# Gated delta heads: another order of the head loop, and the 16x16 block inversion on GpSimd

## The reference, cut to what matters

```
q, k, v = silu(causal conv, width 4, of the projected q, k, v);  q, k unit-norm
decay   = exp(gc_i - gc_j)                     # gc: running sum of the log decay
A       = strict_lower((beta k) k^T * decay)   # in chunks
T       = inverse(I + A)
u = T (beta v);   w = T (beta k exp(gc));   attn = (q k^T) * decay
for each chunk:   v_new = u_c - w_c S
                  o_c   = (q_c exp(gc_c)) S + attn_c v_new
                  S     = S exp(g_last) + (k_c exp(g_last - gc_c))^T v_new
o = gated RMSNorm(o) * silu(z)
```

## Time and profile before

| | |
|---|---|
| median of 3 runs | 2806.33 us (2804.72 to 2807.24) |
| the profiled execution | 2806.93 us, of which the trace's span is 2805.1 us |
| mean granted TensorE clock | 0.915 |
| busy, share of the span | PE 85%, PEld 78%, DVE 40%, ACT 23%, POOL 0.2 us |
| DMA | 191.38 MB, 68 GB/s |

### The profile page before, as it was taken

The page is one execution under the profiler, slowest core; times in us unless marked ns, Lnnn a source line. Parts: engine busy times, 40 slices in busy tenths (PEclk is TensorE's granted clock), DMA queues, the critical chain, the costliest instruction groups (busy, mean ns, idle before and its releaser), DMA issues. The chain is left out here.

```text
span 2805.1 us, 34802 instructions
## 1 busy us (share of the span) xinstructions
PE 2397.6 (85%) x13800; PEld 2184.2 (78%) x13800; DVE 1115.0 (40%) x1922; ACT 638.7 (23%) x1174; POOL 0.2 (0%) x4
## 2 busy tenths in 40 slices
PE   5898985778889898898889667979799999979998
PEld 3686974578878888797878555967699999977676
DVE  4132312535656465655656453334322222231133
ACT  3122312013223131323223110025211111121221
POOL 0000000000000000000000000000000000000000
PEclk9999996579999999999999956989899999989999
DMA  4010210321111111101110044443322222132341
GB/s 153 0 63 16 71 46 16 122 55 50 32 49 38 34 48 32 57 22 50 31 49 16 20 144 140 150 154 113 88 67 67 67 74 68 53 134 54 107 122 57
DMA packets 224158, 191.38 MB, mean 68 GB/s; under 512 B 30253, under 2 KB 197198, under 8 KB 224047
## 3 DMA queue, kind: packets, MB, share of 16 engines
q1 hardware_dynamic: 212792, 152.71, 18.8%
q10 hardware_dynamic: 11302, 37.82, 3.4%
HBM read 138.57 MB, written 52.11 MB: 68 GB/s over the span
## 5 line engine op out<-in xcount | busy, mean ns | idle before, releaser
L271 PE MATMUL bank<-xT_hi,w_lo 128*128 128x344 f32 x1152 | 399.4, 347 | 3.8 <-DVE w_lo L267 3.8
L272 PE MATMUL bank<-xT_lo,w_hi 128*128 128x344 f32 x1152 | 374.1, 325 | 0.0
L273 PE MATMUL bank<-xT_hi,w_hi 128*128 128x344 f32 x1152 | 373.4, 324 | 0.0
L271 PE MATMUL bank<-xT_hi,ffn_lo 128*128 128x344 f32 x1056 | 338.4, 320 | 11.9 <-DVE ffn_lo L267 11.9
L273 PE MATMUL bank<-xT_hi,ffn_hi 128*128 128x344 f32 x1056 | 337.8, 320 | 0.0
L272 PE MATMUL bank<-xT_lo,ffn_hi 128*128 128x344 f32 x1056 | 337.3, 319 | 0.0
L271 PEld LDWEIGHTS bank<-xT_hi,w_lo 128*128 128x128 f32 x1152 | 223.5, 194 | 6.0 <-issue 6.0
L272 PEld LDWEIGHTS bank<-xT_lo,w_hi 128*128 128x128 f32 x1152 | 223.0, 194 | 1.9 <-issue 1.9
L273 PEld LDWEIGHTS bank<-xT_hi,w_hi 128*128 128x128 f32 x1152 | 222.1, 193 | 0.0
L271 PEld LDWEIGHTS bank<-xT_hi,ffn_lo 128*128 128x128 f32 x1056 | 199.2, 189 | 11.9 <-issue 11.9
L273 PEld LDWEIGHTS bank<-xT_hi,ffn_hi 128*128 128x128 f32 x1056 | 199.1, 188 | 0.0
(11 more groups left out here) (377 smaller groups left out, 4158.2 us busy)
## 6 DMA issues: line engine op xcount, KB each, us to landing
w_raw<-in_w_in SPq DMA_DIRECT2D x48, 512.0 KB, 3.9
ffn_raw<-in_w_ffn_in SPq DMA_DIRECT2D x44, 512.0 KB, 5.0
act_scr<-ffn_y ACTq DMA_DIRECT2D x22, 516.0 KB, 2.7
fo_sr<-act_scr SPq DMA_DIRECT2D x16, 704.0 KB, 6.7
fo_wr<-in_w_ffn_out SPq DMA_DIRECT2D x22, 512.0 KB, 5.1
gate_scr<-gate ACTq DMA_DIRECT2D x16, 516.0 KB, 3.7
a_kv_raw<-in_w_in SPq DMA_DIRECT2D x3, 2048.0 KB, 8.6
mix_ta<-gate_scr SPq DMA_DIRECT2D x8, 516.0 KB, 4.8
```

Source lines behind the costliest of these rows:

```text
L271: nc.tensor.matmul(out, stat_lo, mov_hi, start=start, stop=False)
L272: nc.tensor.matmul(out, stat_hi, mov_lo, start=False, stop=False)
L273: return nc.tensor.matmul(out, stat_hi, mov_hi, start=False, stop=stop)
```

## The change

1. **The table and the tiles' order.** `per_slot` becomes 10, 2, 3, 3, 44, 4, three times 6, 4, 2, eight times 4, 18, 4, again 144 steps in sum. The tiles of a head in the loop come as a, q, k, v, b, z. The first tile's weights of the next head are split at the end of the head before (`lo(h + 1, 0)`, `hi(h + 1, 0)`).
2. **The inversion** moves from DVE to GpSimd, with its 28 operations and memset unchanged; GpSimd also clears `ub` at the start. SP's queue has `base_to` ahead of the head's fourth weight load and `base_from` ahead of the sixth.
3. **The norms and the rows.** The squares' sums of q and of the output are taken by ACT (`accum_out`, eight small operations each) in place of DVE's products and sums. The four rb banks come from 16 transposes of a broadcast column in place of four 512-wide products with a diagonal made by DVE, so DVE's two `diag` products go. "an" is made before the last of the four bounds. ACT's tables are loaded ahead by name.
4. **Banks and waits.** The levels' first products use two banks (6, 5) in place of one; the scan has one step in place of two between m1 and m3; `state` is cleared before the levels; `on` comes in two halves; the z silu and `pt` stand later.

```diff
-            per_slot = [20, 4, 8, 8, 28] + LEVELS * [6] + [4] + NT * [4] + [14, 8]
+            per_slot = [10, 2, 3, 3, 44, 4] + LEVELS * [6] + [4, 2] + NT * [4] + [18, 4]
...
-                return 0, NTILE
+                return {0: "a", 1: "q", 2: "k", 3: "v", 4: "b", 5: "z"}
...
                 for n in range(4):
-                    src = (kbe if n < 2 else kdec)[:, 4 * (n % 2):4 * (n % 2) + 4]
-                    inc(nc.tensor.matmul(banks[4 + n][:], ident_ones[:], src.rearrange("p a b -> p (a b)"),
-                                         start=True, stop=True), "rb")
+                    for p in range(4):
+                        c = col[:, 4 if n < 2 else 2, 4 * (n % 2) + p:4 * (n % 2) + p + 1]
+                        last = nc.tensor.transpose(banks[4 + n][:, p * P:(p + 1) * P], c.to_broadcast([P, P]),
+                                                   ident[:])
+                    inc(last, "rb")
...
-                            last = nc.tensor.matmul(banks[6][:, p * P:(p + 1) * P], ea[:, 4 * b + p],
+                            last = nc.tensor.matmul(banks[x_bank[b]][:, p * P:(p + 1) * P], ea[:, 4 * b + p],
                                                     t_sb[b][:, p], start=True, stop=True)
...
-                    fill.upto(done[SCAN + c] - 2)
+                    fill.upto(done[SCAN + c] - 3)
...
-                    inc(nc.scalar.activation(sqb[:].rearrange("p a b -> p (a b)"), banks[5 + b][:],
-                                             ACT.Square), "q_ev")
+                    for p in range(4):
+                        x = banks[5 + b][:, p * P:(p + 1) * P]
+                        last = nc.scalar.activation(x, x, ACT.Square, accum_out=col[:, 1, 4 * b + p:4 * b + p + 1])
+                    inc(last, "q_ev")
...
-                fill.upto(done[BASE] - 16)
-                invert_base(v, nc.vector, i)
...
+                @block.gpsimd
+                def _(pool):
+                    nc.gpsimd.memset(ub[:], 0.0).then_inc(cleared, 1)
+                    with pool.Fori(0, HB) as i:
+                        invert_base(pool, nc.gpsimd, i)
```

More of the change, by code:

```diff
@@ L1781, in project_pe @@
             def project_pe(pe, h, prev):
-                for m in range(*turn_tiles(h)):
+                for m in turn_tiles(h):
                     j, u = m % 2, m // 2
@@ L1796, in project_act, with hi @@
             def project_act(act, h, prev):
-                def hi(m):
+                kind, first, end, more = bounds(h)
+                def hi(h, m):
                     j, u = m % 2, m // 2
@@ L1858, in project_act, with lo @@
                         yield n + 3 * KT
[L1859 to L1860 removed]
+                        hi(h, m + 2)
+                    elif m + 2 == end and more:
+                        yield n + 3 * KT
+                        hi(h + 1, 0)
+                    if x in CONVS:
+                        c = CONVS.index(x)
                         wait(act, evac[2], h, m + 1)
[L1862 to L1863 removed]
+                        inc(nc.scalar.activation(conv_new[:, bass.ds(c * HB + h, 1)],
+                                                 pre[c][:, L:L + 3 + NS].unsqueeze(1), ACT.Copy), "cn")
             def project_dve(v, h, prev):
[L1866 removed]
+                kind, first, end, more = bounds(h)
+                def lo(h, m):
                     j, u = m % 2, m // 2
@@ L2091, in recur_act @@
                     inc(nc.scalar.activation(qe[:, 512 * b:512 * b + 512], banks[6 + b][:], ACT.Exp), "qe_x")
-                for b in range(2):
-                    wt(act, "eq_m", i, b + 1)
                     inc(nc.scalar.activation(eq[:, 4 * b:4 * b + 4], eq[:, 4 * b:4 * b + 4], ACT.Exp), "eq_x")
-                fill.slot(3)
+                wait(act, silu, i, 3); wait(act, evac[2], i, 6)
+                nc.scalar.activation(tanh[:], z_half[:], ACT.Tanh).then_inc(thalf.sem, 1)
                 fill.upto(done[BASE])
@@ L2151, in recur_dve, with bounded @@
                 wt(v, "cols", i, 1)
-                for dst, c in ((kbe, 4), (kdec, 2)):
-                    inc(nc.vector.tensor_tensor(dst[:], ident[:].unsqueeze(1).to_broadcast(F8),
-                                                col[:, c].unsqueeze(2).to_broadcast(F8), ALU.mult), "diag")
-                wait(v, thalf, i, 4)
-                wt(v, "ob", i, 0)
-                nc.vector.scalar_tensor_tensor(zs[:], tanh[:], 1.0, z_half[:], ALU.add,
-                                               ALU.mult).then_inc(silu.sem, 1)
-                fill.slot(2)
-                for n in range(4):
-                    if n == 2:
-                        v.wait_ge(out_dma, 16 + i * 16)
+                def bounded(n):
                     wt(v, "rb", i, n + 1)
@@ L2216, in recur_dve @@
                         w_t[:, 4 * b:4 * b + 4],
-                        banks[4 - b][:].rearrange("p (a b) -> p a b", a=4)), "w_ev")
-                v.wait_ge(st_dma, 16 + i * 16)
-                inc(nc.vector.memset(state[0][:], 0.0), "sm")
+                        banks[3 + b][:].rearrange("p (a b) -> p a b", a=4)), "w_ev")
+                fill.slot(APPLY + 1)
                 wt(v, "u_ev", i, 2)
@@ L2282, in _ @@
                 def _(v):
-                    nc.vector.memset(ub[:], 0.0).then_inc(cleared, 1)
                     constants_take(v)
```

227 lines of the change are left out of this document (119 added, 108 removed).

## The result

The changed kernel takes 2632.5 us (median of 4 runs, 2629.1 to 2636.9), the kernel before 2805.6 in the same session (2804.7 to 2807.2). The ratio is 0.9383, with a 95% interval of 0.9366 to 0.9400. The prediction was 2688 with a range of 2646 to 2775: the direction was right, and the gain of 173 us was half as large again as the 118 forecast. The profiled execution took 2634.9 us, span 2633.2.

A forecast was written before the change was run, and what follows sets the result against it. PE's queue, its work plus its own waits, was taken as the bound. Six loop heads save 91.2 us, the first 9.8, the last 17.2: 118.2 off 2806.93 gives 2688.7, predicted as 2688, range 2646 to 2775.

The forecast's parts named there:

- Which waits go: PE's waits in loop head: silu of v 3.79, bounds 1.18 and `state` 0.92 us gone; levels' 3.45 cut to 0.5.
- The way of the blocks: Inversion's round trip from head start: `base` in place at 20.7 us, X 12.5, 7.0 back; PE's filler ends at 37.1.
- X: Time of the inversion on GpSimd: 12.5 us, the geometric middle of 6.35 (DVE's time) and 24.
- rival 2: GpSimd and DVE hinder each other, adding some 2.5 us to the inversion (X = 15); 2712 us, chance 0.15.
- the clock loss: Behind PE's 3.1 us wait for `ub` in a loop head, half clock loses 1.6 more: 4.7 together.
- rival 1: The 44 steps cover the whole inversion, X at or below 9.4, a head 106.5 us; 2649 us, chance 0.17.
- PE's bare head: PE's loop head without any wait: 105.0 us, from 126.4 less 16.4 waits, 3.7 clock and 1.3 rb.
- The levels (0.5) and the scan (1.0): PE's waits left in a loop head: 0.5 us (0 to 3) in levels, 1.0 (0.3 to 3) in scan.
- The last head: Last head, without filler: 17.2 us saved; 12.9 at the turned blocks, 0.9 `state`, about 2 levels, 1.4 output's norm.
- rival 3: Fillers' new place makes DVE late in levels or scan, 3 us more wait a head; 2709 us, chance 0.10.
- rival 4: Inversion on GpSimd bounds a head, each us of X costing 8 in all; 2864 us at X = 34, slower part 0.06.
- my signs of being wrong: PE waits for `col` at rb, m3 for `vnew` in over four chunks, or GpSimd operations stretch where DVE is busy.

The follow-up runs named there:

- Run 7: Changed kernel with the tiles again in the old order a, b, q, k, v, z: 2691.4 us.
- run 4: Changed kernel with DVE's products for `kbe` and `kdec` moved from beside GpSimd's inversion to just before the first level: 2624.6 us.
- run 5: Changed kernel with six, and in a second kernel fourteen, extra dependent 64x56 products on GpSimd ahead of each inversion: 2678.2 and 2719.7 us.
- run 6: Changed kernel with both halves' first products of the levels sharing bank 6 again, the second waiting for the first's mask: 2640.8 us.
- run 8: Changed kernel with the levels' filler steps back in their old place on PE and DVE, both banks kept: 2640.3 us.
- run 9: Changed kernel with one bank for the levels' first products and the levels' filler steps in their old places, both at once: 2673.4 us.
- Run 1: Changed kernel with the inversion back on DVE, behind the weight split of filler step 24: 2624.5 us.
- run 3: Changed kernel with 47 filler steps in place of 44 ahead of the turned blocks and 15 in place of 18 in the tail: 2624.5 us.
- run 11: Changed kernel with the inversion on DVE, ahead of the products for `kbe` and `kdec`: 2620.5 us.
- run 10: Changed kernel with 42, or 40, filler steps in place of 44 ahead of the turned blocks and 20, or 22, at the head's end: 2653.6, 2685.8 us.
- run 2: Kernel before the change with only the inversion moved to GpSimd: 2819.3 us, ratio 1.0048 to before.

## Why the prediction was right and wrong, point by point

**Which waits go: right.** The silu's wait, the bounds', the levels', and that for `state` left the loop; in the last head two waits of 0.58 us remain in the levels. Run 7 shows the tile order by itself: undone, it brings the silu's wait back with its clock loss.

**The way of the blocks: right to 1 us.** Forecast: `base` in place at t = 20.7, X = 12.5, 7.0 back, PE free at 37.1. Measured: 19.7, 11.9, 7.0 (770.48 to 777.49) and 37.4. The geometric middle of DVE's own speed and a full round an operation came within 5% of X, but by luck in its parts. Without contention the chain takes 9.4 us (run 4), 3.1 less than the forecast's 12.5, which counted little of it, and 1.1 less than the memset's ratio of the earlier trace rows gave. The other 2.5 us are contention, just what rival 2 had counted, but on top of 12.5. Run 4 shows the contention, and run 5 shows it larger (4.5 us for 2.2). The rule of the Trainium skill that was quoted for rival 2 (SBUF — State Buffer, Who interferes with whom) agrees with these rows: 1.07 and 1.16 us beside DVE's two-input operations, 0.21 without them. One thing the forecast did not have: the gate product, with one input, held an operation too (0.56 us in the changed kernel and 0.60 in run 4, where the same shapes take 0.23 and 0.26).

**The step that failed: "PE then waits 3.1 us, and since even 3.79 us brought the half clock for 3.2 us it loses 1.6 more: 4.7."** The wait was 1.12. Three errors of 0.3 to 1.0 us, all to the same side, shrank it: the load was back 1.0 us earlier (4.8 us from "an" to its issue in place of 5.8), X was 0.6 shorter, PE had 0.3 more filler. A wait that is the difference of two large times (20.7 + 12.5 + 7.0 against 37.1) carries all their errors. And the clock loss did not shrink with it but vanished. It goes with the length of the wait: none behind the 35 waits for `ub` in the loops of the changed kernel and of runs 6 to 9 (1.02 to 1.59 us), some at 2.1 us, every one at 4.4 us and more. I charged a loss seen behind 3.79 us to a wait of 3.1 that was itself uncertain by several us; a second case (short wait, full clock) belonged beside it. This step is 3.6 us a head of the 6.9 missed. It does not by itself explain why the result lies below the whole range: rival 1 had this term at zero, and its head was still 106.5. That part is the next two terms.

**PE's bare head, the second step that failed: 105.0 forecast, 103.2 measured** (104.36 - 1.12), 1.8 of the rest. With the 1.5 us of the next paragraph it is what held every case of mine at 106 us a head or more, and the range's lower end at 2646. Where a wait stands, a head loses more than its bracket. Runs 1 and 3 put 0.21 us beside the wait for `ub`, and run 8 puts 0.94 - 0.77 = 0.17 beside its wait. The bracket begins at the modelled end of the product before, and without the wait the next product would start before that end. Six waits went; if each had 0.2 us beside it, which no run shows for them, that is 1.2 us. rb gave 1.7 and not 1.3. The last 0.2 is not assigned.

**The levels (0.5) and the scan (1.0): both zero.** With one step before `vnew`, chunks take 2.78 us and one 3.04, the same as 2.79 and 3.02 before; DVE was ready. In the levels no wait was left. Runs 6, 8 and 9 show why I could not have read that from one edit: bank and steps each suffice nearly alone, and 3.7 us return only when both are undone. My count gave the second bank the credit, and this is wrong for the loop. It was right for the last head, where no steps hide anything: 2.0 us between run 9 and the changed kernel, counted at 2; the 3.7 of run 6 has 1.7 of clock in it.

**The last head: 20.9 saved, 17.2 forecast.** The turned blocks came at 38.3 after the start (forecast 40.2), 1.9 of the 3.7 missed. The way from there to the turned output shrank by 5.5 (forecast 4.3): a wait of 0.83 for `u_sb` at the products for u went that I had not counted, and `state` gave 1.01, not 0.9. The turned output waits 3.31 (forecast 3.4, before 4.80), and what stands behind it took 0.7 less.

**The rivals.** Rival 1 (the steps cover everything) needed X at or below 9.4 and did not come true, though X without contention is just that. Its time of 2649 is the nearest all the same: the result is 16 us below it, since PE's bare head and the small waits were overpriced in it too. Rival 2's mechanism is real at its full price of 2.5 us, on an X that is 3.1 shorter. Rivals 3 and 4 did not come; run 5 confirms rival 4's rule that each us on GpSimd costs a us a head and the clock on top (with fourteen products, 9.1 us of wait for 9.1 more us on GpSimd). Of my signs of being wrong one came true: operations on GpSimd stretch where DVE is busy. What no rival said is that the second half of the change costs time: GpSimd's chain is 3.0 us longer than DVE's 6.35 without contention, 5.5 with it, while DVE (busy 62 of 104 us) had room for it. Run 1 and run 11 are the kernels that leave it out.

**In sum** (a head of the loop, us): 111.2 forecast; 3.6 less for `ub` and its clock, 1.5 less for the levels and the scan, 1.8 less for the bare head; 104.4. Seven heads make 48 us of the 54 between 2688.7 and 2634.9; the last head makes 3.7. The remaining 2 lie outside the heads: 1.6 of them ahead of the first, whose start moves by more than that from one of these traces to another.

## What to carry to other kernels

When one queue sets the time and other engines feed it, ask first in what order the work stands, and only then which engine does it: here all that was not the engine gave about 180 us, undoing the order of the tiles alone costs 59, and the engine took 8 back. Price a clock loss by the length of the wait it follows, with two cases where the wait is uncertain: here 3.1 us of wait would have cost clock, and 1.1 cost none. Before calling an operation's time its own, look at what the neighbour engine does in the same stretch. When two edits both take a wait away, undo both together before giving either the credit.

## What the runs showed of the hardware that I had not expected

- **The same wait can be followed by either clock.** Behind waits of 2.0 to 2.2 us the granted clock fell in two of seven heads in run 10 (42 steps), in five of seven in run 9, in five of six at the heads' starts with 40 steps, and in none of the seven heads of the kernel before, which have a wait of 2.15 in the levels. In run 2, with the same wait at the same place as before, it fell in four of seven. Here are two heads of run 9 with the same work, and two of run 2:

```profile
800.44:803.44 3.00, 3.00 (x13) 3.00 (x14) 0.69 (x1) 0.00 (x0) 0.00 (x0) 0.51 0.59 172
910.13:913.13 3.00, 3.00 (x25) 3.00 (x26) 0.69 (x1) 0.00 (x0) 0.00 (x0) 1.00 0.62 172
```

```profile
714.55:717.55 3.00, 3.00 (x18) 3.00 (x19) 0.69 (x1) 0.00 (x0) 0.00 (x0) 0.69 0.02 5
843.55:846.55 3.00, 3.00 (x24) 3.00 (x25) 1.12 (x2) 0.00 (x0) 0.00 (x0) 1.00 0.00 0
```

  At 2.9 to 3.1 us (run 10, 40 steps) it fell in six of seven, and the one that kept the full clock was the longest, 3.14; at 4.4 us and more in all 14 of run 5. What tells the cases at 2.1 us apart, I did not find out.
- **Small operations on GpSimd are not far from DVE's.** A dependent 64x14 product takes 0.21 us on GpSimd and the 64x56 ones 0.29, at a distance of 0.29 to 0.37; on DVE they take 0.16 to 0.21, at 0.19 to 0.24. The chain of 29 takes about 9.4 us where DVE holds none of it, against 6.35. Beside DVE's long operations on SBUF a single one of them takes up to 1.3 us (run 5, fourteen products).
- **ACT's square with its sum costs less than the two rows add up to.** Each of the eight takes 0.28 us and a read of the accumulator 0.19, but they overlap and follow each other by 0.28. I had counted 0.43.
